# Two of x's eight tiles scaled and added on GpSimd after each branch of a two-layer transformer step

## The reference

```
for l in range(DEPTH):
    h = modulate(rms_norm(x, P['g_pre_mix'][l]), sh1, sc1)
    ...
    x = x + gt1[:, None, :] * rms_norm(mix, P['g_post_mix'][l])
    h = modulate(rms_norm(x, P['g_pre_ffn'][l]), sh2, sc2)
    ...
    x = x + gt2[:, None, :] * rms_norm(f, P['g_post_ffn'][l])
```

## Time and profile before

| | |
|---|---|
| Timed runs | 2177.38, 2178.75, 2180.98 us, median 2178.75 |
| Profiled execution | 2175.0 us, span from first to last instruction 2173.4 us |
| TensorE busy | 1948.1 us, 90% |
| VectorE busy | 419.0 us, 19% |
| ScalarE busy | 335.0 us, 15% |
| GpSimd busy | 50.1 us, 2% |
| Mean granted TensorE clock | 0.919 of full speed |

### The profile page before, as it was taken

One profiled execution on the slowest core, in us unless ns is written; L12 is line 12 of the kernel. 1 busy time (PEld: TensorE's weight loads), 2 busy tenths in 40 slices (PEclk: granted clock), 3 DMA queues, 4 the chain that ended last, 5 costly groups with the idle time before them and its releaser, 6 DMA issues.

```text
span 2173.4 us, 30293 instructions
## 1 busy us (share of the span) xinstructions
PE 1948.1 (90%) x12939; PEld 1424.8 (66%) x12940; DVE 419.0 (19%) x1255; ACT 335.0 (15%) x1000; POOL 50.1 (2%) x96
## 2 busy tenths in 40 slices
PE   6798787998999988997999998899999899999874
PEld 3455565566777745776999654469985499954532
DVE  1104232223000033424110111111001111011113
ACT  2112232222000022432100010100001000011101
POOL 1003011000000000000000000000000000000000
PEclk9996898899999997567999899999998999989997
DMA  9832657552433533042577499997757996849991
GB/s 346 327 138 93 235 209 239 202 194 78 154 105 107 158 110 90 1 152 80 187 275 275 156 398 390 396 392 283 298 205 280 401 365 241 300 166 400 387 399 66
DMA packets 252022, 504.28 MB, mean 232 GB/s; under 512 B 6953, under 2 KB 65497, under 8 KB 251746
## 3 DMA queue, kind: packets, MB, share of 16 engines
q1 hardware_dynamic: 248066, 495.49, 63.3%
q0 software_dynamic: 3808, 6.61, 1.0%
HBM read 499.05 MB, written 3.02 MB: 231 GB/s over the span
## 4 chain that ended last, share of the span: by engine, by line
PE 74%; DMA 11%; SPq 8%; DVE 3%; issue 2%; ACT 1%; POOL 0%; ACTq 0%; DVEq 0%
PE ps L1254 15%; PE ps L1130 8%; PE ps L1304 8%; PE ps L1236 8%; PE ps L738 7%; DMA big<-in_w_moe_out 6%; SPq L573 4%; DMA big<-in_w_ada 3%; PE ps L798 3%; PE ps L1201 3%; PE ps L687 2%; PE ps L1150 2%; DMA big<-in_w_moe_in 2%; SPq L527 1%; PE ps L1332 1%
## 5 line engine op out<-in xcount | busy, mean ns | idle before, releaser
L1254 PE MATMUL ps<-big 128*128 128x144 f32 x2688 | 330.8, 286 | 2.5 <-issue 2.5
L1254 PEld LDWEIGHTS ps<-big 128*128 128x128 f32 x2688 | 329.6, 190 | 3.6 <-issue 3.6
L1236 PE MATMUL ps<-big 128*64 128x256 f32 x2240 | 262.2, 393 | 26.5 <-issue 17.9
L1236 PEld LDWEIGHTS ps<-big 128*64 128x64 f32 x2240 | 161.5, 141 | 117.8 <-issue 34.7
L1130 PE MATMUL ps<-work,big 128*128 128x288 f32 x704 | 172.6, 409 | 4.6 <-ACT work L1394 4.6
L1394 ACT ACTIVATE gqkv<-ps 128x144 f32<-128x144 f32 (+1 forms) x230 | 66.1, 314 | 672.7 <-PE ps L1236 316.5
L1304 PE MATMUL ps<-z,big 128*128 128x144 f32 x1344 | 165.4, 286 | 2.3 <-issue 2.3
L1304 PEld LDWEIGHTS ps<-z,big 128*128 128x128 f32 x1344 | 164.8, 190 | 2.9 <-issue 2.9
L1130 PEld LDWEIGHTS ps<-work,big 128*128 128x128 f32 x704 | 134.7, 191 | 42.5 <-issue 5.0
L1288 PE MATMUL ps<-big,z 128*64 128x512 f32 x560 | 127.7, 598 | 37.7 <-DMA big<-in_w_moe_out 34.6
L2204 DVE TENSOR_TENSOR z<-ps,gqkv 128x256 f32<-128x256 f32 x224 | 69.0, 334 | 451.6 <-ACT gqkv L1394 451.6
(11 more groups left out here) (305 smaller groups left out, 1737.2 us busy)
## 6 DMA issues: line engine op xcount, KB each, us to landing
big<-in_w_moe_in SPq DMA_DIRECT2D x112, 2048.0 KB, 15.6
big<-in_w_moe_out SPq DMA_DIRECT2D x56, 2048.0 KB, 20.1
big<-in_w_ada SPq DMA_DIRECT2D x24, 2048.0 KB, 13.0
big<-in_w_ffd_in SPq DMA_DIRECT2D x22, 1024.0 KB, 7.7
big<-in_w_ffd_out SPq DMA_DIRECT2D x8, 1408.0 KB, 7.1
big<-in_cache_b_k SPq DMA_DIRECT2D x4, 2048.0 KB, 7.9
big<-in_cache_mla_ckv SPq DMA_DIRECT2D x64, 128.0 KB, 2.3
big<-in_cache_b_v SPq DMA_DIRECT2D x4, 2048.0 KB, 10.6
```

The source lines that it names most:

```text
L1236: last = mm(ps[64 * a:64 * a + 64, 512 * b + 256 * g:512 * b + 256 * g + 256], hsel[:, k, 0:NARROW], w[:, k, 256 * a:256 * a + 256], start ...
L1254: last = mm(bank(b, CAP, 256 * g), w[g][:, k, 128 * i:128 * i + 128], hsel[:, k, :], start=(k == 0), stop=(k == KD - 1))
```

## The change

In `post_norm`, VectorE scales and adds tiles 0 to 5; tiles 6 and 7 are scaled and added by GpSimd in a new function `post_norm_last`, called four times in GpSimd's program. The reciprocal raises a new semaphore (`sum_inverted`) for both engines. Whoever needs x's last two tiles waits for GpSimd's own count (`x_updated_by_pool`): ScalarE's squares of these tiles, `pre_norm`, and the second half of the last transposes.

```diff
+KP = 2
+KDV = 8 - KP
...
+            def post_norm_last(m):
+
+                gp.wait_ge(rinv_rdy, m + 1)
+                base = ng[0]
+                for k in range(KDV, KD):
+                    ng[0] += 1
+                    nc.gpsimd.tensor_tensor(fT[:, k, :], fT[:, k, :], rinv[:, :], ALU.mult).then_inc(chain_g, 1)
+                for k in range(KDV, KD):
+                    gp.wait_ge(chain_g, base + k - KDV + 1)
+                    nc.gpsimd.tensor_tensor(xT[:, k, :], xT[:, k, :], fT[:, k, :], ALU.add).then_inc(x_updP, 1)
...
+            post_norm_last(0)
+            post_norm_last(1)
             gp.wait_ge(z_rdy, 11)
             gp.wait_ge(z_cp, 24)
...
+            post_norm_last(2)
+            post_norm_last(3)
             for kk in range(2):
...
-                pe.wait_ge(x_upd, 24 + 4 * kk + 4)
+                pe.wait_ge(x_upd, 3 * KDV + min(4 * kk + 4, KDV))
+                if kk:
+                    pe.wait_ge(x_updP, 4 * KP)
...
-                    act.wait_ge(x_upd, 8 * m + k + 1)
+                    if k < KDV:
+                        act.wait_ge(x_upd, KDV * m + k + 1)
+                    else:
+                        act.wait_ge(x_updP, KP * m + k - KDV + 1)
...
-                    dve.wait_ge(x_upd, 4 * n)
+                    dve.wait_ge(x_upd, KDV * n // 2)
+                    dve.wait_ge(x_updP, KP * n // 2)
...
-                link(V.reciprocal(rinv[:, :], rstd[:, :]))
+                V.reciprocal(rinv[:, :], rstd[:, :]).then_inc(rinv_rdy, 1)
+                dve.wait_ge(rinv_rdy, m + 1)
...
-                for k in range(KD):
-                    if k + 1 < KD:
+                for k in range(KDV):
+                    if k + 1 < KDV:
                         scaled(k + 1)
```

More of the change, by code:

```diff
@@ L328, in build @@
         h_part, h_done, x_upd = sem("h_before_shift"), sem("h_done"), sem("x_updated")
+        x_updP, rinv_rdy, chain_g = sem("x_updated_by_pool"), sem("sum_inverted"), sem("gpsimd_chain")
         ada_done, ada_row, ada_tp, ada_add = sem("ada_done"), sem("ada_rows_copied"), sem("ada_transposed"), sem("ada_added")
@@ L622, in store @@
                 gp.dma_start(dst, src).then_inc(s, 16)
+            ng = [0]
+            def post_norm_last(m):
[7 more added lines that the diff above has]
+                    nc.gpsimd.tensor_tensor(xT[:, k, :], xT[:, k, :], fT[:, k, :], ALU.add).then_inc(x_updP, 1)
             gp.wait_ge(z_rdy, 5)
```

## The result

| | median, us | runs |
|---|---|---|
| the kernel before | 2177.46 | 20 |
| the changed kernel | 2188.41 | 20 |

The ratio is 1.0049, 95% interval 1.0036 to 1.0061: the change makes the kernel slower by some 11 us (8 to 13). The profiled execution has a span of 2185.2 us, 11.8 above that of before.

What follows compares the result with a forecast made beforehand. TensorE, busy 90%, bounds the kernel; only its waits for VectorE count. Branches 0 to 2 at +2.1 each (+6.3) and branch 3 at +2.7 make +9.0: 2175.0 to 2184.0, plus 3.75 for the median, 2188; range 2177 to 2195.

Steps and rivals of the forecast that it cites:

- Where the path runs: Branches 0 to 2: only the first addition is on the chain of waits; instructions removed from VectorE are worth 0.
- Turns, one each: In each branch VectorE and GpSimd instructions alternate, each holding the other off for its length; together +9.0 us, chance 0.55.
- The length h: Length of one GpSimd 128x288 instruction in the edited step, taken as 0.74 us, twice VectorE's spacing of 0.37.
- the same working: Sum with alternating engines: first addition moves 1.48 us, later ones 2.96; sums of branches 0 to 2 end 10.5 against 8.43.
- The clock: Sums of branches 0 to 2: clock rises from 0.50 5.15 us after the first matmul; +2.1 each, +6.3 together.
- one of the signs by which I had said that I would be wrong: The clock of the sums rises at another point than 5 us after their start.
- My other case: Sums of branches 0 to 2: clock rises 5.15 us after the second start, ending at 11.6, +3.2 each.
- Branch 3: Last transposes: the fourth addition moves by 2.96 us and the 0.24 wait for the second half goes; +2.7.
- From execution to median: Whole kernel: 3.75 us added to the profiled execution's forecast 2184.0, since the three timed runs' median lay that far above it.
- Free running: Rival: both engines work side by side unhindered, VectorE's spacing stays 0.37, branch 3 gains 0.24; -0.2 us, chance 0.26.
- GpSimd last: Rival: VectorE's next instruction always goes first, GpSimd's four follow; +0.3 three times, +1.45 at the end, together +2.3; chance 0.12.
- GpSimd too slow alone: Rival: no interference, but GpSimd's instructions take 1.95 us and finish late; 0.8 three times, 1.9 at the end, +4.3; chance 0.03.

Runs made afterwards that it cites:

- Run 2: The kernel before, with four idle GpSimd additions (two inputs, constant into spare memory) after each reciprocal, nobody waiting for them: 2187.11 us, ratio 1.0044.
- run 3: The kernel before, with four idle GpSimd memsets (no input) after each reciprocal: 2182.72 us, one execution.
- run 1: The changed kernel, with GpSimd's four instructions waiting until VectorE has made its sixth addition: 2180.1 us, ratio 1.0029.
- run 6: The changed kernel, with the inverted vector copied to PSUM and VectorE's scalings reading it there: 2171.31 us, one execution.
- run 11: The changed kernel with VectorE's scalings reading the inverted vector from a PSUM copy, run again with timing: 2176.25 us, ratio 0.9994.
- 9: The kernel before, with nine dummy 128x256 matmuls in each TensorE pause around the sums and ahead of the last transposes: 2172.04 us, ratio 0.9979.
- run 10: The changed kernel, with twelve dummy matmuls ahead of the sums, nine behind them and fourteen in branch 3: 2177.87 us, ratio 1.0012.
- 4: The kernel before, with four idle GpSimd copies (one input) after each reciprocal: 2167.26 us, one execution.
- run 5: The changed kernel, with only tile 7 on GpSimd and seven tiles on VectorE: 2179.97 us, ratio 1.0020.

## Why the prediction came out right, step by step

The prediction was 2188.0 us, range 2177 to 2195, with 0.56 on slower; measured were 2188.4 and a clear slowdown. The mechanism is the forecast one, but two sizes were off in opposite directions.

- **Where the path runs.** Held. In the kernel before, the additions behind the first are not on the chain, so the four instructions taken from VectorE gave back nothing in branches 0 to 2; in branch 3 the 0.24 us of wait between the halves went, as forecast.
- **Turns, one each.** Held: four long instructions a branch, alternating with GpSimd's. Run 2 shows that GpSimd's additions alone do it, on whatever data, run 3 that its writes alone don't, run 1 that the hold goes when the two don't overlap, and runs 6 and 11 that a scaling without its second SBUF input isn't held.
- **The length h.** I took 0.74 for a GpSimd instruction and used it for two things. As its own length it was right (0.76 alone, run 1; the estimate of 0.63 from the Trainium skill, GPSIMD Engine Reference, section 3.1, was below that). As the time for which it holds VectorE it was too large: 0.60. Hence the start at 2.92 instead of 3.21 and the second tile at 4.85 instead of 5.43; with 0.60 the same working gives 2.93 and 4.87.
- **The clock.** I let it rise 5.15 us after the first matmul, as before; it rose after 6.6 to 7.5, one of the signs by which I had said that I would be wrong. My other case, as long after the second start, was nearer (4.7, 4.8 and 5.5 against 5.15); with a hold of 0.60 its working gives +2.65 a branch, 8.0 for the three. With a hold of 0.60 and the rise where I had it, the same working gives an end at 10.14, +1.7; with a hold of 0.60 and branch 0's measured rise it gives 10.87, and 10.83 was measured. This is the step that failed; the too long hold hid about half of it. Measured were +2.4, +2.7 and +2.8, together +7.9 instead of +6.3.
- **Branch 3.** +2.7 forecast, +2.86 measured, by a shorter hold (2.4 us for the fourth addition, not 2.96) and a slower end: TensorE's transposes stay at the low clock, 5.38 us for both halves, 0.7 more than before without its wait.
- **From execution to median.** +9.0 against the profiled execution was too small by 2.8; the 3.75 us that I added, because that execution lay below its three timed runs, were too much: over 20 runs the kernel before has 2177.46. The two errors nearly cancel, so the 0.4 us by which the median was met are luck in part.
- **The rivals.** Free running fell with the first timeline. GpSimd last is what run 1 makes by a wait; it costs there nearly twice what the working gave, +0.6, +0.8 and +0.6 in the branches and +2.3 at the end, where +0.3 and +1.45 were forecast. GpSimd too slow alone needed h above 1.44; it is 0.76.

What stays open: the 1160 us between branches 2 and 3 took 1155.5 to 1163.4 in the thirteen profiles, whatever the kernel, so how much of a branch's delay is kept through that stage can't be read from one execution. In the pair 9 and 10 the distance from branch 2 to branch 3 differs by 0.6 us only, though the sums of branch 2 end 1.9 later.

## What to carry to other kernels

Before work goes from VectorE to GpSimd, look at whether the two will run side by side on SBUF data: if so, VectorE's own instructions get longer, unless one of their inputs can lie in PSUM (here the scalings' factor, for a copy of 0.44 us a branch), and the first of them may be the only one on the path. Price an offload at the instruction that the next engine waits for, not by the sum of the work taken away. And a short step between two TensorE stages can cost twice when it gets longer: once as a wait, and once through the clock behind it.

## What the runs showed of the hardware that I had not expected

- GpSimd's 128x288 fp32 addition takes 0.76 us alone and holds a VectorE instruction with two SBUF inputs by 0.60; a copy holds it by 0.22, a memset not at all (runs 1 to 4).
- A VectorE scaling with one of its two inputs in PSUM is not held beside GpSimd (0.45 us, run 6), and with its scalings reading PSUM the changed kernel takes the time of the kernel before (run 11, 0.9994).
- Around the sums of the runs without dummies the clock stayed at 0.50 for 6.8 us in twenty branches and for 10.2 us in seven. In run 5 the sums of the branch with 10.2 end at 10.10, those of the two with 6.8 at 8.84 and 9.42.
- The granted clock fell to 0.50 behind an idle time of 1.18 us in one branch and stayed at 1.00 behind the same idle time in two others of the same execution (run 10).
- Dummy matmuls that keep TensorE from idling ahead of a stage pay for themselves here: 0.9979 (0.9966 to 0.9992) for the kernel before with nine in each pause, since the sums then run at 1.00 and end at 7.39 instead of 8.43.
